# Moving four memory-token products within the written-out order of a transformer kernel

## The chip, the cores and the metric

The kernel runs on one core of one Trainium2 chip. The metric is the device time of one execution in microseconds (us). The core has five engines that each work through their own instruction stream in program order: PE (TensorE, matrix products), DVE (VectorE), ACT (ScalarE), POOL (GpSimd) and SP (SyncE, here the queue that issues the loads). They meet only at semaphores.

## What is computed

A first block takes x (256 tokens, 1024 features): root-mean-square norm, one wide input projection, and three branches from it: a latent attention (8 heads, ranks 384 and 256, rotary part of 32), a decaying attention ("fox", 8 heads of 64) and a state-space scan (16 heads of 64, after a short convolution). Gates, an output projection and a convolved feed-forward follow. A second block of two layers follows, whose memory attention uses keys and values of 256 memory tokens. These depend on the inputs alone. In the reference:

```python
def memory_kv(mem, mem_norm, w_mem_kv):
    b, m, _ = mem.shape
    k, v = jnp.split(rmsnorm(mem, mem_norm) @ w_mem_kv, 2, axis=-1)
    return (k.reshape(b, m, N_MEM_HEADS, HEAD_DIM), v.reshape(b, m, N_MEM_HEADS, HEAD_DIM))
```

and the latent attention's up-projection, with the norm and the rotation of each head:

```python
    q = (rms_norm(c_q, q_norm_g) @ w_uq).reshape(Bsz, S, MLA_HEADS, MLA_QK_DIM)
    kv = (rms_norm(c_kv, kv_norm_g) @ w_ukv).reshape(Bsz, S, MLA_HEADS, MLA_NOPE + MLA_V)
    q = rope_tail(rms_norm(q, q_gain), cos, sin)
    k = rope_tail(rms_norm(k, k_gain), cos, sin)
```

Only the time at which the four memory products (keys and values of two layers) are formed is touched.

## The kernel before

Everything is held feature-major, 128 partitions by chunks times 256 tokens. The function `order` writes out one list of steps, `STEPS`. Every engine's program is a walk through that same list (L1079 for PE, L1431 for ACT, L1858 for DVE, L717 for SP), so the list fixes each engine's own order, and semaphores fix the rest. A step ("g", stage, i) is a product group, which fills one of four PSUM banks. The others are: "sq" squares on ACT, "ns" and "nm" the norm's sums on PE, its `Ln` and `Exp` on ACT and its application on DVE, "rope" the rotation (one product on PE, three DVE operations), "trig" the sine table (18 short dependent DVE operations in `angles_` at L1531, then a `Sin` on ACT at L1436 and the reload of the function table), "A", "B", "C", "D" the phases of an attention head.

Each group's weights, mostly 1 MB, come through `ring`, four slots (`load`, L693). SP issues the load of number n in the order of the list, and only once slot n - 4 is free. Two kinds of groups exist. For the stages in `SPLIT` (the input projections "min", "fqk", "fv", "xbc", "z" and others) the weights are first split into a high and a low part, `w_hi` on ACT (L1154) and `w_lo` on DVE (L1497), two buffers of each, and the product is three matmuls for one (`three`, L769, matmuls at L779). The slot is free once `w_lo` is made. For the rest ("uq", "uk", "uv", "memkv") the matmuls read `ring` itself (L810, L819, L874), and the slot is free only once the group is done.

Where a split stands in the streams of ACT and DVE is decided by `split_before` (L414): at the group in which its buffer comes free, that is at the last use of the split two before it. If the slot four loads back belongs to a group that isn't split, it stands no earlier than two groups behind that one:

```python
        g = LAST[BY_SPLIT[n - 2]] if n >= 2 else -1
        before = BY_LOAD.get(LOAD[key] - RING)
        if before is not None and before not in SPLITS:
            g = max(g, min(LAST[before] + 2, GROUP_OF[key] - 1))
```

In a group's turn ACT and DVE make the splits first and then empty the bank. For "xbc" the splits come behind the linear part and the taps of the convolution (L1214, L1609).

Around the change the list is: norms of x and of the memory, "min" 0 and 1 and "min2" (latent inputs), memory product 0, "trig", memory products 1 to 3, squares of the query latent ("sq cq"), "fqk" 0, its norm ("nm cq"), and so on through "fqk" 3 and "fv" 1, then the up-projection: ten groups "uq" 0 to 3, "uk" 0 to 3, "uv" 0 and 1 (variable `up`), with the norm of group t - 1 and the rotation of group t - 2 behind group t. After it come the fox heads, each with one "xbc" or "z" group behind it. On PE, "nm cq" waits for the squares of ACT, which stand behind "trig" in ACT's stream. The memory groups' banks are emptied by ACT (L1193), those of "uq" and "uk" by DVE (L1576).

Of the kernel before, what the change touches and what calls it, by code (L numbers as in the profile page):

```python
# [243 lines left out]
def order():  # L244

    def norm(name):  # L250

        return [(k, name, i) for i in range(4) for k in ("sq", "ns")] + [("nm", name)]

    def late(name, groups):


        per = len(groups) // 4
        out = []
        for i in range(4):
            out += groups[per * i:per * i + per] + [("sq", name, i)]  # L260
            if i:
                out.insert(len(out) - 1 - (per > 1), ("ns", name, i - 1))
        return out

    def down(n):
        return [("g", f"down{n}", c) for c in range(KC)]

    st = norm("x1") + [("g", "fdt", 0)]
    st += [("g", "min", 0), ("ft",)] + norm("mem") + [("g", "min", 1), ("g", "min2", 0)]
    st += [("g", "memkv", 0), ("trig",)] + [("g", "memkv", n) for n in range(1, 4)]  # L270
    st += [("sq", "cq"), ("g", "fqk", 0), ("nm", "cq"), ("sq", "ckv"), ("g", "fqk", 1), ("nm", "ckv")]
    st += [("sq", "f0"), ("g", "fqk", 2), ("nm", "f0"), ("sq", "f1"), ("g", "fqk", 3), ("nm", "f1")]
    st += [("sq", "f2"), ("g", "fv", 0), ("nm", "f2"), ("sq", "f3"), ("g", "fv", 1), ("nm", "f3")]

    up = [("g", "uq", n) for n in range(4)] + [("g", "uk", n) for n in range(4)]
    up += [("g", "uv", 0), ("g", "uv", 1)]
    for t, g in enumerate(up):
        st += [g] + ([("sq", f"m{t}")] if t < 8 else []) + ([("nm", f"m{t - 1}")] if 1 <= t <= 8 else [])
        st += [("rope", t - 2)] if t >= 2 else []

    def ticks(heads, fill):

        n = len(heads)
        out = [("G", *heads[0])]
        for t in range(n + 2):
            out += [("A", *heads[t])] if t < n else []
            out += [("D", *heads[t - 2])] if t >= 2 else []
            out += [("C", *heads[t - 1])] if 1 <= t <= n else []
            out += [("B", *heads[t])] if t < n else []
            out += [("E", *heads[t - 1])] if 1 <= t <= n else []  # L290
            out += [("G", *heads[t + 1])] if t + 1 < n else []
            out += fill(t)
        return out

    first = [("g", "xbc", n) for n in range(6)] + [("g", "z", n) for n in range(2)]
    st += ticks([("fox", h) for h in range(FOX_H)], lambda t: first[t:t + 1])
    st += [("cb", 0), ("cb", 1)]

    fill = [("g", "z", 2), ("g", "z", 3)] + [(("g", "gate", 4 + n), ("g", "brf", n))[m] for n in range(4) for m in (0, 1)]
    st += ticks([("mla", h) for h in range(8)], lambda t: fill[t:t + 1] + ([("xt", t)] if t < 4 else []))  # L300
    rest = [(("g", "gate", n), ("g", "brm", n))[m] for n in range(4) for m in (0, 1)]
    rest += [("g", "gate", n) for n in range(8, 12)]

    def ssd_fill(t):

        out = rest[t:t + 1]
        for i in range(4):
            if t == max(4 * i + 5, len(rest) + i):
                out += [("sq", "ssm", i)] + ([("ns", "ssm", i)] if i < 3 else [])
        return out  # L310

    st += ticks([("ssd", h) for h in range(SSM_H)], ssd_fill)
    st += [("g", "brs", 0), ("ns", "ssm", 3), ("nm", "ssm")] + [("g", "brs", n) for n in range(1, 4)]
    st += late("ffn1", [("g", "out1", n) for n in range(4)]) + [("nm", "ffn1"), ("ffn", "1")]
    st += late("mixa", down("1"))

    st += [("g", "qma", 0), ("ns", "mixa", 3), ("nm", "mixa")] + [("g", "pool", n) for n in range(4)]
    wg = [("g", "wg", n) for n in range(4)]
    st += ticks([("mema", h) for h in range(4)], lambda t: wg[t:t + 1])
    st += late("ffna", [("g", "outa", n) for n in range(KC)]) + [("nm", "ffna"), ("ffn", "a")]  # L320
    st += late("mixb", down("a"))

    st += [("g", "kk", 0), ("ns", "mixb", 3), ("nm", "mixb"), ("g", "qq", 0), ("rt",), ("g", "kv", 0)]
    more = [("g", "kk", 1), ("g", "qq", 1), ("g", "kv", 1), ("g", "kk", 2), ("g", "qq", 2),
            ("g", "kv", 2), ("g", "qmb", 0)]
    heads = [("sb", h) for h in range(12)] + [("memb", h) for h in range(4)]
    st += ticks(heads, lambda t: more[t:t + 1])
    st += late("ffnb", [("g", "outb", n) for n in range(4)]) + [("nm", "ffnb"), ("ffn", "b")]
    st += late("last", down("b")) + [("ns", "last", 3), ("nm", "last")]
    return st  # L330


STEPS = order()


# [1638 lines left out]
```

## Time and profile before

| what | value |
|---|---|
| median of 3 runs | 1327.72 us (1326.32 to 1330.77) |
| span of the profiled execution | 1326.9 us, 21884 instructions |
| PE busy | 1243.7 us, 94% |
| DVE busy | 745.5 us, 56% |
| ACT busy | 602.3 us, 45% |
| mean granted PE clock | 0.970 of full |

The span runs from the first to the last instruction of one execution. Busy times of PE are modelled at their ends, so that the pitch (start to start) of its groups tells more than the length of one. The page's chain of work follows back from the last instruction to what released each step.

### The profile page before, as it was taken

The page shows a single profiled execution, that of the slowest core. Times are in us where ns is not written, and L with a number is a line of the kernel's source. Part 1 is how long each engine was busy: PE and PEld are TensorE (multiplying, and loading weights), DVE is VectorE, ACT ScalarE, POOL GpSimd, SP SyncE. Part 2 cuts the span into 40 slices and gives each one's busy share as a digit, 9 for nine tenths or more (in the row PEclk, how much of TensorE's full clock was granted, in tenths as well). Part 3 has the DMA queues.
Part 4 walks back from the last instruction along what each step waited for, and adds up shares of the span by engine and source line. Part 5 has one row for each costly group of instructions (what it writes and reads, how often), then busy time and mean ns, then how long its engine had stood idle before and what let it go on. Part 6 is the DMA issues. An engine that isn't in the chain of part 4 may idle for free.

```text
span 1326.9 us, 21884 instructions
## 1 busy us (share of the span) xinstructions
PE 1243.7 (94%) x8910; PEld 1138.8 (86%) x8910; DVE 745.5 (56%) x1167; ACT 602.3 (45%) x930; POOL 127.8 (10%) x118
## 2 busy tenths in 40 slices
PE   5899899889997999998998999999999989999996
PEld 4798378778896999888997799999999758999996
DVE  3424678543544768887547247775555333677643
ACT  4346355443333565554451254444566633544333
POOL 0000011000432015554000000000000000000000
PEclk8899899999998999999998999999999979999998
DMA  7152143213351444444551265544554104555451
GB/s 270 67 204 92 53 152 103 96 49 143 124 194 64 155 161 163 158 164 134 173 182 51 90 232 191 183 159 160 194 194 145 43 1 147 203 188 179 134 180 49
DMA packets 29789, 186.56 MB, mean 141 GB/s; under 512 B 3312, under 2 KB 3568, under 8 KB 13456
## 3 DMA queue, kind: packets, MB, share of 16 engines
q1 hardware_dynamic: 29712, 185.46, 40.0%
q8 instruction: 57, 0.93, 0.3%
q14 instruction: 20, 0.16, 0.0%
HBM read 184.40 MB, written 1.05 MB: 140 GB/s over the span
## 4 chain that ended last, share of the span: by engine, by line
PE 76%; DVE 9%; ACT 7%; issue 6%; DMA 1%; DVEq 0%; ACTq 0%; POOL 0%; POOLq 0%; SPq 0%
PE bank L779 54%; PE bank L810 6%; DVE acc L1832 3%; ACT w_hi L1154 3%; PE bank L909 3%; DVE w_lo L1497 3%; PE S L959 2%; PE O L1071 2%; PE T L1045 1%; PE bank L819 1%; PE O L1075 1%; ACT xh L1266 1%; PE S L1014 1%; PE S L1038 1%; PE S L986 1%
## 5 line engine op out<-in xcount | busy, mean ns | idle before, releaser
L1497 DVE TENSOR_TENSOR w_lo<-ring,w_hi 128x1024 fp32r<-128x1024 f32 (+4 forms) x338 | 369.1, 1133 | 281.3 <-ACT w_hi L1154 281.2
L779 PE MATMUL bank<-xh,w_hi 128*128 128x256 f32 (+2 forms) x1736 | 496.5, 286 | 16.1 <-DVE w_lo L1497 7.7
L779 PE MATMUL bank<-xl,w_hi 128*128 128x256 f32 (+2 forms) x1736 | 488.8, 282 | 0.0
L779 PE MATMUL bank<-xh,w_lo 128*128 128x256 f32 (+2 forms) x1736 | 488.6, 281 | 0.0
L1154 ACT ACTIVATE w_hi<-ring 128x1024 fp32r<-128x1024 f32 (+4 forms) x338 | 309.5, 964 | 348.3 <-PE bank L779 343.8
L779 PEld LDWEIGHTS bank<-xh,w_hi 128*128 128x128 f32 (+2 forms) x1736 | 325.9, 188 | 23.2 <-issue 14.7
L779 PEld LDWEIGHTS bank<-xl,w_hi 128*128 128x128 f32 (+2 forms) x1736 | 326.0, 188 | 0.9 <-issue 0.2
L779 PEld LDWEIGHTS bank<-xh,w_lo 128*128 128x128 f32 (+2 forms) x1736 | 325.8, 188 | 0.4
L779 PE MATMUL bank<-hid_hi,w_hi 128*128 128x256 f32 x528 | 150.8, 286 | 3.0 <-POOL hid_lo L1932 2.1
L779 PE MATMUL bank<-hid_lo,w_hi 128*128 128x256 f32 x528 | 149.0, 282 | 0.0
L779 PE MATMUL bank<-hid_hi,w_lo 128*128 128x256 f32 x528 | 148.9, 282 | 0.0
L779 PEld LDWEIGHTS bank<-hid_hi,w_hi 128*128 128x128 f32 x528 | 100.3, 190 | 3.7 <-POOL hid_lo L1932 2.3
L779 PEld LDWEIGHTS bank<-hid_lo,w_hi 128*128 128x128 f32 x528 | 100.3, 190 | 0.2
L779 PEld LDWEIGHTS bank<-hid_hi,w_lo 128*128 128x128 f32 x528 | 100.3, 190 | 0.0
L1822 DVE TENSOR_TENSOR acc<-bank,rstd 128x512 f32<-128x512 f32 x44 | 30.4, 691 | 48.4 <-PE bank L779 48.4
L959 PE MATMUL S<-sqr,cst 128*128 128x256 f32 x128 | 37.9, 434 | 16.5 <-ACT sqr L1285 16.5
L1266 ACT ACTIVATE xh<-x,cst,par 128x256 fp32r<-128x256 f32 x40 | 21.8, 592 | 64.3 <-DVE x L1652 35.1
L1832 DVE SCALAR_TENSOR_TENSOR acc<-pr,par,acc 128x255 f32<-128x255 f32 (+1 forms) x88 | 46.5, 568 | 3.0 <-DVE acc L1832 0.2
L959 PEld LDWEIGHTS S<-sqr,cst 128*128 128x128 f32 x128 | 26.7, 221 | 20.9 <-issue 9.7
L1415 ACT ACTIVATE sg<-acc,cst 128x256 f32<-128x256 f32 x22 | 11.2, 510 | 62.9 <-DVE acc L1832 62.9
L1932 POOL TENSOR_TENSOR hid_lo<-sg,hid_hi 128x256 f32 (+1 forms) x22 | 32.2, 1464 | 3.5 <-POOL hid_hi L1930 3.4
L1652 DVE TENSOR_TENSOR x<-x,bank 128x256 f32<-128x256 f32 x32 | 13.3, 416 | 31.9 <-PE bank L909 25.3
(262 smaller groups left out, 1570.1 us busy)
## 6 DMA issues: line engine op xcount, KB each, us to landing
ring<-w_up SPq DMA_DIRECT2D x22, 1024.0 KB, 4.8
ring<-w_upa SPq DMA_DIRECT2D x22, 1024.0 KB, 4.9
ring<-w_upb SPq DMA_DIRECT2D x22, 1024.0 KB, 4.9
ring<-w_gate SPq DMA_DIRECT2D x12, 1024.0 KB, 5.7
ring<-w_down SPq DMA_DIRECT2D x16, 704.0 KB, 4.2
ring<-w_downa SPq DMA_DIRECT2D x16, 704.0 KB, 4.1
ring<-w_downb SPq DMA_DIRECT2D x16, 704.0 KB, 4.1
ring<-w_xbc SPq DMA_DIRECT2D x6, 1024.0 KB, 4.9
```

What stands on the lines that cost most here:

```text
L779: last = mm(out, lhs, rhs, start=(k == 0 and (a, b) == (0, 0)), stop=(whole and k == ks[-1] and (a, b) == (1, 0)))
L810: last = mm(b[p0:p0 + width, m * S:m * S + S], W[0:kp, k * wide + c0:k * wide + c0 + width], src(k), start=(k == 0), stop=(k == kc - 1))
L909: last = mm(banks[g % RING][:, 0:S], W[0:p, k * P:(k + 1) * P], src, start=(k == 0), stop=(k == 9))
L959: last = mm(b[:, 0:S], C("ones"), sqr[:, ((i % 2) * 2 + c) * S:((i % 2) * 2 + c + 1) * S], start=(i == 0 and c == 0), stop=(i == 3 and c = ...
L1071: mm(o[:, 0:S], v[:, 0, :], p[:, 0:S], start=True, stop=False)
L1154: A(w_hi[:, q % 2, a:e], raw[:, a:e], ACT.Copy).then_inc(hi_ready, 1)
L1266: last = A(hi[:, c, :], src[:, c, :], ACT.Identity, bias=C("zero"), scale=Pm(gain, c))
L1497: last = V.tensor_tensor(w_lo[:, q % 2, a:e], raw[:, a:e], w_hi[:, q % 2, a:e], ALU.subtract)
L1652: V.tensor_tensor(x[:, i, :], x[:, i, :], b[:, 0:S], ALU.add).then_inc(free, 1)
L1822: V.tensor_tensor(y.rearrange("p (a t) -> p a t", a=2), bank[:, :].rearrange("p (a t) -> p a t", a=2), factor(S), ALU.mult).then_inc(free, 1)
L1832: ins = stt(part, y[:, m * S:(m + 1) * S - late], par[:, bass.ds(j * 8 + o, 1)], part, ALU.mult, ALU.add)
L1932: Q.tensor_tensor(lo, h, hi, ALU.subtract).then_inc(up_hid, 1)
```

## The change

The four memory groups leave their place between "min2" and "sq cq", and only "trig" stays there. They stand now in the up-projection, one behind the rotation step of every even t below 8, that is behind "uq" 0, "uq" 2, "uk" 0 and "uk" 2. Nothing is added or removed.

```diff
     st += [("g", "min", 0), ("ft",)] + norm("mem") + [("g", "min", 1), ("g", "min2", 0)]
-    st += [("g", "memkv", 0), ("trig",)] + [("g", "memkv", n) for n in range(1, 4)]
+    st += [("trig",)]
     st += [("sq", "cq"), ("g", "fqk", 0), ("nm", "cq"), ("sq", "ckv"), ("g", "fqk", 1), ("nm", "ckv")]
@@
     for t, g in enumerate(up):
         st += [g] + ([("sq", f"m{t}")] if t < 8 else []) + ([("nm", f"m{t - 1}")] if 1 <= t <= 8 else [])
         st += [("rope", t - 2)] if t >= 2 else []
+        st += [("g", "memkv", t // 2)] if t % 2 == 0 and t < 8 else []
```

Load numbers, ring slots, bank numbers and the places of the splits follow from the list by the same functions.

## Rows read from the trace of the kernel before

**Rows 1.** The page: its span, and its chain by engine.

```profile
span 1326.9 us, 21884 instructions
...
PE 76%; DVE 9%; ACT 7%; issue 6%; DMA 1%; DVEq 0%; ACTq 0%; POOL 0%; POOLq 0%; SPq 0%
```

**Rows 2.** Stretches of 10 us: busy time (instructions) by engine, PE clock, DMA share, GB/s.

```profile
140.00:150.00 10.00, 7.08 (x18) 2.57 (x18) 5.91 (x8) 3.68 (x6) 0.00 (x0) 0.73 0.22 91
...
260.00:270.00 10.00, 8.81 (x61) 8.43 (x62) 3.31 (x9) 3.62 (x10) 0.00 (x0) 0.83 0.32 105
```

**Rows 3.** Chain of work in order of time, 0 to 200 us: start, length, what.

```profile
57.61 6.91 PE bank L810 x32
...
85.23 5.63 PE bank L779 x48
90.86 1.29 PE S L760 x6
...
125.04 5.19 PE bank L810 x24
...
147.53 0.69 DVE mqk L1576
...
153.20 0.69 DVE mqk L1576
...
171.90 0.97 PE S L1092 x2
...
183.44 5.63 PE bank L779 x48
```

**Rows 4.** Timeline of the up-projection, PE: start, length, line, tiles.

```profile
135.43 2.83 PE L810 MATMUL bank<-xbc,ring 128*96 128x256 f32 x12
...
138.10 1.02 PE L974 MATMUL S<-sqr,cst 96*96 96x512 f32 x2
...
139.06 1.04 PE L1092 MATMUL S<-mqk,cst 32*32 32x512 f32 x2
...
140.03 1.94 PE L810 MATMUL bank<-xbc,ring 128*64 128x256 f32 x8
```

**Rows 5.** Timeline of DVE: first and last of 18 angle operations, one split.

```profile
50.72 0.42 DVE L1536 CAST acc<-sg 32x512 f32<-32x512 int32 x1
...
60.06 0.42 DVE L1554 TENSOR_SCALAR merged<-merged 32x512 f32<-32x512 f32 x1
...
98.98 2.36 DVE L1497 TENSOR_TENSOR w_lo<-ring,w_hi 128x1024 fp32r<-128x1024 f32 x2 [3.25 <-ACT w_hi L1154]
```

**Rows 6.** Timeline of ACT: the sine, squares of the query latent, one split.

```profile
65.17 1.28 ACT L1436 ACT_TABLE_LOAD   x1
66.46 1.14 ACT L1436 ACTIVATE merged<-merged,cst 32x1024 f32<-32x1024 f32 x1
67.62 1.28 ACT L1135 ACT_TABLE_LOAD   x1
...
85.77 0.93 ACT L1280 ACTIVATE sqr<-xbc,cst 128x768 f32<-128x768 f32 x1
...
97.88 2.01 ACT L1154 ACTIVATE w_hi<-ring 128x1024 fp32r<-128x1024 f32 x2 [1.34 <-PE bank L779]
```

**Rows 7.** Timeline of ACT behind the first state-space group.

```profile
183.77 1.28 ACT L1216 ACT_TABLE_LOAD   x1
```

**Rows 8.** Timeline of DVE behind the first state-space group: taps, then a split.

```profile
181.97 2.69 DVE L1604 SCALAR_TENSOR_TENSOR acc<-bank,halves,acc 128x255 f32<-128x255 f32 x6 [3.65 <-ACT acc L1211]
184.57 2.35 DVE L1497 TENSOR_TENSOR w_lo<-ring,w_hi 128x1024 fp32r<-128x1024 f32 x2
```

**Rows 9.** Timeline of PE: its restart after an idle stretch.

```profile
39.55 6.73 PE L959 MATMUL S<-sqr,cst 128*128 128x256 f32 x16 [5.13 <-ACT sqr L1285]
```

**Rows 10.** Stretches of 1 us, PE: length, busy (instructions), granted clock, DMA share, GB/s.

```profile
39.00:40.00 1.00, 0.45 (x1) 0.50 0.69 270
...
45.00:46.00 1.00, 1.00 (x6) 0.66 0.00 0
```

**Rows 11.** Loads issued from 78 to 86 us: count, KB each, median us to landing.

```profile
ring<-w_fqk SPq DMA_DIRECT2D x2, 1024.0 KB, 4.9
ring<-w_fv SPq DMA_DIRECT2D x1, 1024.0 KB, 7.0
```

## The prediction, as it was put on record before the kernel ran

> **What bounds the kernel now.** I read the page's chain first. PE holds 76% of a span of 1326.9 us, and DVE, ACT and issue share nearly all the rest [rows 1]. So a change pays where PE isn't the one that is waited for. The chain in order of time gives those places for the stretch that is edited. From 57.61 to 85.23 it is PE alone, back to back: the four memory products, 6.91 us each [rows 3]. Then "fqk" and "fv" follow without a wait (5.63 us a group, 1.29 for the sums of "nm cq"), until the up-projection starts at 125.04 [rows 3]. There the chain leaves PE. It goes round through DVE's emptying of a bank, ACT's square, `Ln` and `Exp`, DVE's scaling and its three rotation operations, and back to the next emptying: 147.53 to 153.20 is one turn, 5.67 us [rows 3]. The stretches agree: from 140 to 150 PE was busy for 7.08 of 10 us, at a granted clock of 0.73 [rows 2]. The last rotation is at 171.90, 0.97 long, so the up-projection lasts 172.87 - 125.04 = 47.8 us [rows 3]. This is the idle time of PE that the change fills. Four things have to be priced.
>
> **1. What leaves the front.** The memory products were on the chain for 85.23 - 57.61 = 27.6 us [rows 3]. Without them "fqk" 0 can start at 57.61. Its weights are there: the loads of "fqk" take the ring turns that the memory loads had, and these were issued long before. Its split now stands at "min" 1 (its slot and its buffer are free by then), so `w_lo` is made well before 57.61. Gain: -27.6.
>
> **2. What the memory products covered.** They stood beside "trig". Now "trig" has two splits ahead of it on DVE and only one group of PE beside it. DVE's stream is static: split of "fqk" 0 at "min" 1, split of "fqk" 1 at "min2", and then the angles. The second waits for the product of "min2", which still reads the buffer, so it begins at 57.61. A split takes 3.46 us from the start of `w_hi` to the end of `w_lo` (97.88 on ACT to 98.98 + 2.36 on DVE) [rows 5, 6], so the angles start at 61.07 instead of 50.72. They take 60.48 - 50.72 = 9.76 us [rows 5] and end at 70.83. ACT then has the sine, 1.14, the reload of its table, 1.28, and the squares of the query latent, 0.93 [rows 6]: 74.2. With a semaphore's 0.1 PE gets its sums "nm cq" at 74.3. It had finished "fqk" 0 at 57.61 + 5.63 = 63.24, and "nm cq" is next in its stream, ahead of "fqk" 1. **PE stands still for 11.1 us.** Queued behind ACT's wait for the angles are those squares, the split of "fqk" 2 and the emptying of "fqk" 0; none of them is later than PE once PE moves again. The first of the two table loads I count as hidden: at 183.77 ACT began such a load although the taps that its `Tanh` waits for ended only at 181.97 + 2.69 = 184.66 [rows 7, 8], so a load is made ahead of the wait. Were it behind the wait, 1.3 us more.
>
> The Trainium skill's page ScalarE: Activation LUTs ("What ACT_TABLE_LOAD costs") gives about 2.66 us for a switch, a drain included. The trace doesn't bear out the drain, for the sine follows its load by 0.01 us [rows 6]; by the page the sum would be 1.4 us more for the reload.
>
> Then the clock. After an idle time of 5.13 us PE restarted at 39.55, with a granted clock of 0.50 [rows 9, 10], that is 1.2 GHz, and had 2.4 GHz again in the course of the stretch 45 to 46 (0.66) [rows 10]. That is 6.2 us at half speed, 3.1 us lost. An idle time of 11.1 us is longer, so I take the same loss, with 0 and 3.4 as ends. Cost of part 2: +11.1 + 3.1 = +14.2.
>
> **3. The up-projection with the memory products in it.** First PE's work alone, by pitches at full clock. "uq" takes 138.10 - 135.43 = 2.67, a norm's sums 139.06 - 138.10 = 0.96, a rotation 140.03 - 139.06 = 0.97, "uk" about 1.90 [rows 4], "uv" the same. The sum is 4 x 2.67 + 6 x 1.90 + 8 x 0.96 + 8 x 0.97 + 4 x 6.91 = 65.2 us. This is above 47.8: PE becomes the bound, and the idle time takes up only 10.2 of the 27.6 us.
>
> Then what PE still waits for, from its start at 0, by the same durations. While "uq" goes, nothing: each memory product gives the DVE and ACT turn more than its 5.67 us. "uq" 3 ends at 27.4. It frees a ring slot, so memory load 3 is issued and right behind it that of "xbc" 0, at 27.75. Two loads that close landed after 4.9 and 7.0 us [rows 11], so "xbc" 0 is there at 34.8. Its split now stands in the turn of "uk" 0, ahead of the emptying of that bank (two groups behind memory product 1, whose slot it takes). ACT waits there for the load, and behind it on ACT are the squares of "uk" 0 and the norm before it, on DVE the emptying of "uk" 0. The split ends at 38.25. Emptying, square, `Ln`, `Exp` and scaling (0.7 each) end at 41.9 and the first rotation operation at 42.6. PE meanwhile has "uk" 0, sums, a rotation and memory product 2, until 40.05, and "uk" 1 until 41.95. So this wait of some 5 us is nearly all covered. Going on, PE waits 0.3 us for the sums behind "uk" 2 and 1.25 us for the rotation before memory product 3, as the turn of "uk" 1 has no product beside it; near the end 0.2 more. In all 1.9 us, and 67.1 us for the stretch: 67.1 - 47.8 = **+19.3**. Bounds: 65.2 with no wait (+17.4), and 2.6 us more where "xbc" 0 lands later (9.6 us, had two loads been ahead of it), +22. PE is then busy for 65.2 of 67.1 us, more than in either stretch of [rows 2] where the clock fell, so I keep its full clock.
>
> **4. The fox heads' start.** Before, the split of "xbc" 1 lay in the up-projection's turn. Now its load waits for the slot of the "uk"/"uv" weights, free at the end of "uv" 1, and `split_before` puts its split at "xbc" 0, behind the taps. There the trace has a split already (of "xbc" 2): taps at 181.97, `w_lo` from 184.57 to 186.92 [rows 8]. That place is taken by "xbc" 1's. PE was at "xbc" 1 at 183.44 [rows 3], so it now waits 186.9 - 183.4 = **+3.5 us**. The load, issued a little ahead of 172.9 in the old time, lands by about 179, before ACT wants it at 181.8. "xbc" 2's split follows, 2.35 later, and PE wants it only 9 us on. Ends: 0, if DVE's order left room (it doesn't), and +1.7 more if the idle time lets the clock fall for a while, as in the stretch 260 to 270, with PE busy for 8.81 us and a clock of 0.83 [rows 2] (1.7 of 10 us, twice, at half speed). From "xbc" 3 on, loads, splits and banks stand as before, so the rest only shifts.
>
> **Sum.** -27.6 + 14.2 + 19.3 + 3.5 = +9.4 us. On the profiled execution: 1326.9 + 9.4 = 1336.3. The median of the runs shown is 0.8 above that span, so the prediction is **1337.1 us**, 0.7% slower.
>
> **The rivals.**
> - *The clock costs nothing at the restart, or less.* Then +6.3 us, 1334.0. Against it: the restart at 39.55. Chance 0.12.
> - *The middle is worse.* ACT's wait for "xbc" 0 comes out through PE, because the loads share the DMA engines with memory load 3 (+2.6), the clock falls once there or at "xbc" 1 (+1.7), and the sine's table load is behind the wait (+1.3): +15.0, 1342.7. For it: three small bounds that all point one way. Chance 0.15.
> - *Faster: PE isn't held at "nm cq".* This is the one mechanism that changes the sign. The angles, sine, reload and squares take 9.76 + 1.14 + 1.28 + 0.93 + 0.1 = 13.2 us, and hide if they start by 63.2 - 13.2 = 50.0. With part 2 at nothing the sum is -27.6 + 19.3 + 3.5 = -4.8, 1322.9. It needs the angles to be ahead of both splits on DVE; in the list they are behind "min2". Chance 0.07.
> - *The change does what it says in full:* the up-projection stays at 47.8 us, with its idle time holding all products. Then -27.6 + 14.2 + 3.5 = -9.9, 1317.8. PE's own 65.2 us speak against it. Chance 0.02.
>
> The forecast has 0.62; 0.02 are left for what I don't see.
>
> **How the numbers follow.** The forecast's own bounds (clock 0 to 3.4, up-projection +17.4 to +22, fox start up to +5.2, table load 0 to 1.3) reach from about 1332 to 1343, and the first two rivals lie inside. The range is 1330 to 1343; outside it are the two faster cases and small tails. What a measurement of this kernel can tell from no change is about 0.3%, 4 us. Faster by more has the last rival and nearly all of the one before it: 0.07. Within 0.3%, that is up to 1331.7, needs most of the bounds at their low ends at once, or a part of the stall at "nm cq" gone: 0.10. Slower has 0.83.
>
> **What would show it.** In the profile of the changed kernel PE should stand idle for 11 us before the sums of "nm cq" (L760), near 63 to 74 us, released by ACT's squares; the angles on DVE should start near 61. The granted clock should be 0.50 for some 6 us after that. From the first "uq" to the first fox scores it should be near 67 us, with PE busy nearly throughout, ACT waiting for the load of "xbc" 0 by the split's line, and the memory products at 6.9 us each. At the second "xbc" group there should be an idle time of 3.5 us, released by `w_lo`. The prediction is wrong if the angles are ahead of the splits on DVE, if the up-projection is far from 67 us, or if a later stage changes its length by more than 1 us.

## The result and the profile after

| | kernel before | changed kernel |
|---|---|---|
| median of 6 runs each | 1328.99 us | 1339.74 us (1337.68 to 1346.26) |
| ratio | | 1.009, 95% interval 1.006 to 1.012 |
| span of the profiled execution | 1326.9 us | 1338.2 us |
| mean granted PE clock | 0.970 | 0.966 |

The change makes the kernel slower by 0.9%, 10.8 us by the medians. 1337.1 us was forecast, which is 9.4 us above the median of 1327.72 us that the kernel before had at that time; three more runs of it brought that median to 1328.99. The spans differ by 11.3 us. All line numbers of kernel.py behind the edit are one higher than before. The page has PE's share of the chain as it was [rows 1]:

```profile
span 1338.2 us, 21884 instructions
...
PE 76%; DVE 10%; ACT 7%; issue 5%; DMA 1%; DVEq 0%; ACTq 0%; POOL 0%; SPq 0%; POOLq 0%
```

The chain of work in order of time, 0 to 205 us (start, length, what), answers to [rows 3]:

```profile
44.69 11.35 PE bank L780 x96
56.12 1.07 ACT w_hi L1155
57.22 2.36 DVE w_lo L1498 x2
59.61 0.43 DVE acc L1537
...
68.95 0.43 DVE merged L1555
70.56 1.28 ACT L1136
71.86 0.94 ACT sqr L1281
72.84 2.93 PE S L761 x6
75.77 6.57 PE bank L780 x48
82.34 0.86 PE S L761 x4
...
109.41 12.09 PE bank L811 x56
...
175.99 0.42 PE S L999 x2
...
190.21 7.41 PE bank L780 x48
```

PE ends "min2" at 44.69 + 11.35 = 56.04. The chain then leaves PE: it goes through the split of "fqk" 1, the angles, the sine, the reload of the table and the squares, and comes back to PE only at 72.84. "fqk" 0 isn't on it at all. From there PE holds it up to the up-projection, which lasts from 109.41 to 175.99, 66.6 us against 47.8 before.

The timeline of PE has the two idle times and who ended them, in the brackets at the end of each line:

```profile
72.84 2.93 PE L761 MATMUL S<-sqr,cst 128*128 128x256 f32 x6 [11.18 <-ACT sqr L1281]
...
190.21 0.42 PE L780 MATMUL bank<-xh,w_hi 128*128 128x256 f32 x1 [3.63 <-DVE w_lo L1498]
```

The timeline of ACT has both waits that the prediction named, for the angles and for the load of "xbc" 0:

```profile
60.31 1.28 ACT L1437 ACT_TABLE_LOAD   x1
69.40 1.14 ACT L1437 ACTIVATE merged<-merged,cst 32x1024 f32<-32x1024 f32 x1 [7.81 <-DVE merged L1555]
...
143.79 2.01 ACT L1155 ACTIVATE w_hi<-ring 128x1024 fp32r<-128x1024 f32 x2 [4.45 <-DMA ring<-w_xbc]
```

Here the sine's table load, at 60.31, ends 7.8 us ahead of the sine itself: a load is made ahead of the wait, as [rows 7, 8] let expect. The stretches of 1 us of PE (length, busy, granted clock, DMA share, GB/s) answer to [rows 10]:

```profile
64.00:65.00 1.00, 0.00 (x0) 0.53 0.00 0
...
77.00:78.00 1.00, 1.00 (x8) 0.64 0.85 230
...
189.00:190.00 1.00, 0.00 (x0) 1.00 0.00 0
190.00:191.00 1.00, 0.79 (x4) 0.68 0.00 0
191.00:192.00 1.00, 1.00 (x7) 0.50 0.77 205
...
193.00:194.00 1.00, 1.00 (x7) 0.61 1.01 393
```

The clock went to 1.2 GHz (0.50) some 2.4 us into the long idle time, which began at 61.7, and was back at 2.4 GHz only behind 77. Behind the short idle time it fell too, in the stretch from 190 to 191 in which PE restarted, and was back behind 193.

### The profile page after: what moved, and what is told of

The parts are those of the page before. It is cut to its first block, busy times and chain, and to the rows that moved or that the text cites. A ratio compares the mean times of both kernels' runs of the same rounds, so it can differ in the third digit from the quotient of the medians.

```text
span 1338.2 us, 21884 instructions
## 1 busy us (share of the span) xinstructions
PE 1244.0 (93%) x8910; PEld 1142.4 (85%) x8910; DVE 745.5 (56%) x1167; ACT 602.9 (45%) x930; POOL 128.9 (10%) x118
## 4 chain that ended last, share of the span: by engine, by line
PE 76%; DVE 10%; ACT 7%; issue 5%; DMA 1%; DVEq 0%; ACTq 0%; POOL 0%; SPq 0%; POOLq 0%
PE bank L780 54%; PE bank L811 6%; DVE acc L1833 3%; DVE w_lo L1498 3%; ACT w_hi L1155 3%; PE bank L910 3%; PE S L960 2%; PE O L1072 2%; PE bank L820 1%; PE T L1046 1%; PE O L1076 1%; PE S L1015 1%; ACT xh L1267 1%; PE S L1039 1%; PE S L975 1%
## 5 line engine op out<-in xcount | busy, mean ns | idle before, releaser
L1416 ACT ACTIVATE sg<-acc,cst 128x256 f32<-128x256 f32 x22 | 11.2, 511 | 62.7 <-DVE acc L1833 62.7
```

## The experiments

Each time is a median, each ratio is to the kernel before, run on the same chip, and the brackets behind a ratio are its 95% interval. The diffs show edits against the changed kernel (for e5 and e7: against e1); "..." marks what is left out.

**e1_trig_early** moves the sine step ahead of "min" 1 and with it the application of the memory's norm behind "min" 1. It leaves the memory products where the change put them.

```diff
-    st += [("g", "min", 0), ("ft",)] + norm("mem") + [("g", "min", 1), ("g", "min2", 0)]
-    st += [("trig",)]
+    st += [("g", "min", 0), ("ft",)] + norm("mem")[:-1] + [("trig",), ("g", "min", 1)]
+    st += [("nm", "mem"), ("g", "min2", 0)]
```

> The changed kernel, but the sine table's step is put between the memory norm's last sums and min 1, and the memory norm's application behind min 1, so that on DVE the 18 angle operations stand ahead of both splits and in a stretch in which DVE has nothing to do (about 40 to 47 us). My theory (PE stands still for 11.2 us at the sums of nm cq because ACT's squares wait behind the sine and the sine behind the angles, and then loses 2.6 us of clock): both go, and the time falls by about 13.8 us against the changed kernel, to 0.998 of the kernel before. Rival (the 11 us are owed to the weights of fqk, which the memory products gave time to be split): the wait stays and is released by w_lo, time within 3 us of the changed kernel, 1.008.

Measured: 1322.79 us, ratio 0.9959 (0.9931 to 0.9986). DVE's timeline has the first angle operation at 40.13, and the chain (start, length, what) runs through the place of the idle time on PE:

```profile
46.47 16.96 PE bank L780 x144
63.43 1.29 PE S L761 x6
64.73 5.70 PE bank L780 x48
...
97.61 12.09 PE bank L811 x56
...
178.38 7.49 PE bank L780 x48
```

"min" 1, "min2" and "fqk" 0 are 144 matmuls without a gap, the sums of "nm cq" follow at once, at full clock (1.29 us against 2.93). From the restart at 46.47 to the start of the sums are 16.96 us, against 72.84 - 44.69 = 28.15 in the changed kernel: the 11.2 us are gone. The rival falls. With the sine's cost removed the change gains. By the ratios this kernel is 1.3% (17 us) below the changed one where 13.8 us had been expected; the two intervals cover the difference.

**e6_one_product_left** is the same cause in another dose.

```diff
-    st += [("trig",)]
+    st += [("g", "memkv", 0), ("trig",)]
...
-        st += [("g", "memkv", t // 2)] if t % 2 == 0 and t < 8 else []
+        st += [("g", "memkv", t // 2)] if t in (2, 4, 6) else []
```

> The changed kernel with one memory product left in its old place ahead of the sine step, the other three behind uq 2, uk 0 and uk 2. My theory: that product gives PE 6.9 us of work while the angles run, so the idle time at the sums of nm cq shrinks from 11.15 to about 4.2 us, us for us, and the clock loss of 2.6 us behind it mostly goes; the up-projection gets 6.9 us shorter, less about 0.5 for the turn of uq 0; the idle time at xbc 1 stays at 3.65 us. That is -6.9 (idle) -2.6 (clock) and +0.5: 8 to 9 us below the changed kernel, 1.002 to 1.003 of the kernel before. Rival (the idle time has a fixed cause): it stays near 11 us.

Measured: 1328.83 us, ratio 1.0033 (1.001 to 1.0056). The timeline of PE:

```profile
74.13 2.93 PE L761 MATMUL S<-sqr,cst 128*128 128x256 f32 x6 [4.28 <-ACT sqr L1281]
```

6.91 us of work put back took 11.18 - 4.28 = 6.90 us from the idle time. The clock part of the expectation was wrong: the sums still took 2.93 us, so an idle time of 4.28 us cost as much clock as one of 11.18. This is the plainest test of what the products covered, since one product moved back is its whole edit. The up-projection took 59.7 us (60.2 expected).

**e4_block_before_up** keeps the front and undoes the interleaving.

```diff
+    st += [("g", "memkv", n) for n in range(4)]
     up = [("g", "uq", n) for n in range(4)] + [("g", "uk", n) for n in range(4)]
...
-        st += [("g", "memkv", t // 2)] if t % 2 == 0 and t < 8 else []
```

> The changed kernel without the interleaving: all four memory products in one block directly ahead of the first uq group. The front is as in the changed kernel, the up-projection as in the kernel before, and the slot order of xbc as before. My theory: only the front's 13.8 us are left as a cost, about 1.010 to 1.011 of the kernel before, with an up-projection of 47.8 us and no idle time at xbc 1; so the interleaving by itself gains 27.6 - 18.75 = 8.85 us and gives 5.4 back at xbc 1, and this kernel is about 2.5 to 3 us slower than the changed one. Rival (interleaving gains nothing, because a turn with a product in it makes ACT and DVE late): this kernel is as fast as the changed one or faster.

Measured: 1342.27 us, ratio 1.010 (1.0063 to 1.0138). Its chain:

```profile
111.03 6.91 PE bank L811 x32
...
138.68 4.75 DMA ring<-w_xbc
...
189.43 0.42 PE S L999 x2
...
200.02 5.70 PE bank L780 x48
```

Block and up-projection last from 111.03 to 189.43, 78.4 us, against 66.6 interleaved. So the interleaving takes 11.8 us off, more than the 8.85 expected, since the block has a cost that I had overlooked: "xbc" 0 now follows memory product 3 in its slot, and ACT waits for that load in the turn of "uq" 1 with nothing beside it. As expected, the second "xbc" group starts 200.02 - 189.43 = 10.6 us behind the first fox scores and not 14.2. The times don't settle which of the two kernels is slower: they weren't run beside each other, and the intervals of their ratios (1.0063 to 1.0138, 1.006 to 1.012) overlap. The traced execution of e4 even ended at 1334.1 us, 4.1 us ahead of that of the changed kernel, though it was some 8 us behind when it ended "xbc" 1 (200.02 + 5.70 against 190.21 + 7.41). Its granted clock was higher later on, 0.93 against 0.76 between 1050 and 1100 us. So the 11.8 us are shown for that stretch, by one trace of each, and not in the time of the whole kernel.

**e2_products_earlier** asks what the idle time at "xbc" 1 comes from. Memory products 2 and 3 stand behind "uq" 3 and "uk" 2.

```diff
-        st += [("g", "memkv", t // 2)] if t % 2 == 0 and t < 8 else []
+        st += [("g", "memkv", (0, 2, 3, 6).index(t))] if t in (0, 2, 3, 6) else []
```

> The changed kernel, but memory products 2 and 3 behind uq 3 and uk 2 (steps t = 0, 2, 3, 6 instead of 0, 2, 4, 6). The uk/uv weights then load one turn later, and the slot that xbc 1 needs is that of memory product 2, free early: its split moves back into the up-projection. My theory (the 3.65 us of idle time at the second xbc group, and 1.8 us of low clock behind it, come from that slot): they go, -5.4 us, and the up-projection gets some 2.6 us longer, as its turns with uk 0 and uk 1 have no product beside them and one more split: -2.8 us in all against the changed kernel. Rival (the wait at xbc 1 is DVE's load in the fox heads, wherever the slot comes from): no change there, +2.6 us.

Measured: 1343.06 us, ratio 1.0108 (1.0067 to 1.0148), a miss. Its chain, then the timeline of PE in its up-projection, then that of DVE in the fox heads:

```profile
163.97 9.55 PE bank L820 x32
...
194.62 5.71 PE bank L780 x48
204.18 2.28 DVE w_lo L1498 x2
206.59 7.39 PE bank L780 x48
```

```profile
159.84 1.07 PE L975 MATMUL S<-sqr,cst 96*96 96x512 f32 x2 [2.52 <-ACT lnv L1307]
```

```profile
204.09 4.63 DVE L1498 TENSOR_TENSOR w_lo<-ring,w_hi 128x1024 fp32r<-128x1024 f32 x4
```

The idle time at "xbc" 1 is gone (194.62), but one of the same kind stands at "xbc" 2, which is the one that now follows the uk/uv weights in their slot. The rule of `split_before` puts that split two groups behind "uv" 1, together with that of "xbc" 3 (four halves in one row). And the up-projection took 72.4 us, 5.8 more than in the changed kernel, where 2.6 had been expected: two turns without a product, those of "uk" 0 and "uk" 1, let PE idle, the clock fell, and memory product 3 took 9.55 us, not 7.1. The rival, which had seen no change at "xbc" 1, falls all the same.

**e3_both** has the edits of e1 and e2.

> Both edits: the sine table's step early, and the memory products at t = 0, 2, 3, 6. If both theories hold and the two add, -16.6 us against the changed kernel: 0.996 to 0.997 of the kernel before. If only the first holds, 0.999 to 1.000; if neither, 1.010.

Measured: 1329.51 us, ratio 1.0008 (0.9983 to 1.0032). This is near what had been expected if only the first theory holds (0.999 to 1.000). It is 13.5 us below e2, where the sine's part was put at 13.8. In the trace the sums of "nm cq" have no idle time, as in e1, and the up-projection takes 72.3 us, as in e2 (72.4). So the two parts don't disturb each other; against e1 the time is 6.7 us higher by the medians.

**e5_tail** frees the uk/uv slot early in another way, on top of e1.

```diff
-    up += [("g", "uv", 0), ("g", "uv", 1)]
+    between = {0: ("g", "memkv", 0), 2: ("g", "memkv", 1), 5: ("g", "uv", 0), 6: ("g", "uv", 1)}
...
-        st += [g] + ([("sq", f"m{t}")] if t < 8 else []) + ([("nm", f"m{t - 1}")] if 1 <= t <= 8 else [])
+        st += [g, ("sq", f"m{t}")] + ([("nm", f"m{t - 1}")] if t else [])
...
-        st += [("g", "memkv", t // 2)] if t % 2 == 0 and t < 8 else []
+        st += [between[t]] if t in between else []
+    st += [("g", "memkv", 2), ("nm", "m7"), ("rope", 6), ("g", "memkv", 3), ("rope", 7)]
```

> e1_trig_early with the up-projection laid out anew: memory products 0 and 1 behind uq 0 and uq 2, the two value groups uv behind uk 1 and uk 2 (they have no norm of their own and so fill turns), memory products 2 and 3 behind uk 3 with the last norm and the last two rotations between and behind them. The slot of the uk/uv weights is then free two groups before xbc 0, and the split of xbc 1 moves to memory product 3. My theory (the idle time at the fox heads' start follows the slot of xbc 1 and split_before's two groups): no idle time at xbc 1 or xbc 2, which saves 3.65 us and 1.8 us of low clock; the up-projection gets 2 to 4 us longer, since the uk turns have less beside them. 1 to 3.5 us below e1_trig_early, 0.993 to 0.995 of the kernel before. Rival (any split more in the up-projection costs as much there): 0.996 to 0.998.

Measured: 1325.2 us, ratio 1.0006 (0.9987 to 1.0026). Timeline of PE, then the chain:

```profile
135.64 1.99 PE L976 MATMUL S<-sqr,cst 96*96 96x512 f32 x2 [5.46 <-ACT lnv L1308]
```

```profile
123.01 6.97 DMA ring<-w_xbc
...
173.44 5.69 PE bank L781 x48
181.77 5.63 PE bank L781 x48
190.99 5.70 PE bank L781 x48
```

No idle time at "xbc" 1 or 2 (pitches 8.3 and 9.2 us, as before). But the up-projection took 75.6 us, 9.0 more than the 66.6 of e1, where 2 to 4 had been expected, and so the time is a miss (0.993 to 0.995 expected). What had covered ACT's wait for the load of "xbc" 0 was memory product 2 behind "uk" 0. Without it the load stands on the chain and the wait comes out on PE, 5.46 us, with a low clock behind it. This supports, from the other side, the cover in part 3 of the prediction; e5 moves other groups too, so it isn't a test of that product alone.

**e7_split_free_first** leaves the order of e1 and changes only where the split of "xbc" 1 stands: in the turn of "xbc" 0, ahead of the emptying of the bank and not behind the taps. `splits` takes the list of splits as `keys` for it; DVE's stream has the same edit as ACT's. In the turns of the other "xbc" groups the rule moves nothing.

```diff
+def split_xbc(g, free):
+    return [key for key in SPLIT_AT.get(g, []) if (LAST[BY_SPLIT[SPLITS[key] - 2]] < g) == free]
...
-                if stage != "xbc":
-                    splits(GROUP[stage, i])
+                splits(GROUP[stage, i], keys=split_xbc(GROUP[stage, i], True) if stage == "xbc" else None)
...
-                        splits(GROUP[stage, i])
+                        splits(GROUP[stage, i], keys=split_xbc(GROUP[stage, i], False))
```

> e1_trig_early with one edit more: in the turn of an xbc group, a split whose buffer is free already (that of xbc 1, in the turn of xbc 0) stands ahead of the emptying of the bank, and only the others stay behind the taps. My theory (PE's 3.65 us of idle time at xbc 1 come from the place of its split behind taps that it doesn't depend on, and the low clock behind it from that idle time): w_lo of xbc 1 is ready by the end of the product of xbc 0, the idle time falls to 0 to 0.5 us, the up-projection stays at 66.6 us, and 4 to 5.4 us go against e1_trig_early: about 0.992 of the kernel before. Rival (the load of xbc 1, which waits for the slot of the uk/uv weights, lands too late): the idle time stays above 2 us, released by the DMA through w_hi.

Measured: 1319.61 us, ratio 0.9934 (0.9909 to 0.996). The timeline of DVE and the chain:

```profile
170.02 2.36 DVE L1502 TENSOR_TENSOR w_lo<-ring,w_hi 128x1024 fp32r<-128x1024 f32 x2 [0.20 <-ACT w_hi L1160]
173.26 2.69 DVE L1609 SCALAR_TENSOR_TENSOR acc<-bank,halves,acc 128x255 f32<-128x255 f32 x6 [0.88 <-ACT acc L1216]
```

```profile
166.46 5.63 PE bank L785 x48
174.73 5.70 PE bank L785 x48
184.01 5.70 PE bank L785 x48
```

The split is made while PE is still in "xbc" 0, and "xbc" 1 starts at 174.73, 8.3 us behind the start of "xbc" 0, at full clock. The load wasn't late: ACT had begun `w_hi` by 168.94. This version is faster than both kernels, by 0.7% against the kernel before.

**e1_again** ran on the same chip as e7.

> e1_trig_early once more on the chip of e7_split_free_first, so that the two can be compared at the same state. 0.996 of the kernel before, as it was. Idle time at xbc 1 3.65 us.

Measured: 1326.09 us, ratio 0.9971 (0.9947 to 0.9994). So e7's edit is worth some 5 to 6.5 us by the times (the ratios and the medians), 5.4 by the traces (idle time 3.6, product 7.45 against 5.70 us). The intervals of the two ratios overlap.

**before_again and after_again** give a second trace of each kernel.

> The kernel before once more, for a second trace. The trace of the changed kernel has 2.8 us more than the kernel before between 262 and 285 us, at identical work, where its granted clock is low for some 7 us more. If that belongs to the change, this trace shows the same clock there as the first (low for 3 us between 250 and 300). If it is chance, the low stretches differ from the first trace's, and the span with them.

> The changed kernel once more, for a second trace. Everything up to the second xbc group should repeat within 1 us (idle time of 11.15 us, up-projection of 66.6 us, idle time of 3.65 us). If the 2.8 us behind it are chance, the clock between 258 and 308 us is low for another length than the 10 us of the first trace.

Measured spans: 1321.3 and 1333.5 us, one execution each, against 1326.9 and 1338.2 in the first traces: both are some 5 us shorter at the same instructions. The difference of the two kernels is 12.2 us here and was 11.3. In after_again the up-projection, from 111.04 on, and the start of "xbc" 1, at 191.89 with 7.46 us, repeat the first trace. The start of "min" 1 doesn't: it was 1.6 us earlier in the changed kernel (44.69 against 46.28) and is 1.5 us later here (46.03 against 44.48). The stretch from 250 to 300 us (length, busy, clock, DMA share, GB/s), in before_again, after_again, e1_trig_early and e1_again, one fence each:

```profile
250.00:300.00 50.00, 43.47 (x298) 0.95 0.15 54
```

```profile
250.00:300.00 50.00, 41.05 (x273) 0.90 0.15 53
```

```profile
250.00:300.00 50.00, 43.46 (x303) 0.97 0.19 70
```

```profile
250.00:300.00 50.00, 43.46 (x279) 0.90 0.16 55
```

The two traces of the changed kernel agree (0.90 both), so they alone would have spoken for a cost of the change. The two traces of e1 don't: one kernel has 0.97 and 0.90 there. In all twelve traces of this case 0.90 stands in four: both of the changed kernel, e1_again and e6. The other eight have 0.93 to 0.97, among them the first of e1 and that of e7, which have the memory products in the same places. So the change doesn't fix the value, but it may well make the lower one more frequent; the runs leave this open.

What makes the second traces shorter lies mostly further on. The stretch from 1050 to 1100 us, in before, before_again, after and after_again:

```profile
1050.00:1100.00 50.00, 41.30 (x153) 0.80 0.00 0
```

```profile
1050.00:1100.00 50.00, 41.61 (x170) 0.86 0.06 21
```

```profile
1050.00:1100.00 50.00, 43.52 (x185) 0.76 0.00 1
```

```profile
1050.00:1100.00 50.00, 40.30 (x207) 0.93 0.02 7
```

The kernel before has 0.80 and 0.86 there, the changed one 0.76 and 0.93, each at nearly the same place in its work. So a few us of difference between two spans can come from there.

## Why the prediction was right

Point by point, changed kernel against kernel before, in us of the first profiled executions:

| step of the prediction | forecast | measured |
|---|---|---|
| 1. products out of the front | -27.6 | -27.6; "min2" also ended 1.6 earlier (56.04 against 57.61) |
| 2. PE idle at the sums of "nm cq" | +11.1 | +11.2 |
| 2. low clock behind it | +3.1 | +2.6 (72.84 to 82.34 is 9.5; 1.29 + 5.63 before [rows 3]) |
| 3. up-projection | +19.3 | +18.8 (66.6 against 47.8) |
| 4. PE idle at "xbc" 1 | +3.5 | +3.6 |
| 4. low clock behind it | 0, bound 1.7 | +1.8 (7.41 against 5.63) |
| the rest | 0 | +2.5 (remainder to 11.3); it arises between 250 and 300 us, with the low clock there |

**The mechanism of each term held.** The angles started at 59.61, 1.5 us ahead of the 61.07 forecast, because "min2" ended 1.6 earlier. The first table load was hidden. The reload took 1.28 us, and the squares began 0.02 us behind its end (70.56 and 71.86), so no drain is seen here either. ACT waited for the load of "xbc" 0, and product 2 covered it; e5 shows what it costs uncovered. The two bounds of step 3 (+17.4 and +22) hold the measured +18.8, near the lower: 66.6 us are 1.4 above PE's own 65.2, and not 1.9. The one wait of PE in the stretch is 1.2 us, for the rotation ahead of memory product 3, where the prediction had put 1.25; its two smaller waits, 0.3 and 0.2, didn't come.

**What was mis-sized is the clock.** I took full clock behind the idle time at "xbc" 1 and put the loss into a bound; it came in the changed kernel, in its second trace, and in both of e1. e6 adds that 4.28 us of idle time cost the full 2.6 too. With the measured 1.8 as the likeliest value the forecast would have been 1338.9, nearer to the 1339.74 measured; another 1.3 us is the median of the kernel before, which was 1327.72 with three runs and 1328.99 with six. The 1.6 us at the front come from ahead of the change: the restart of PE that [rows 9] show at 39.55 came at 38.45, and its sums took 6.24 us, not 6.73. They are chance, for the second pair of traces has the sign the other way (1.5 us later).

**One of its own signs of being wrong came true.** The prediction called itself wrong if a later stage changed its length by more than 1 us. In the first pair of traces the part behind "xbc" 1 is 2.8 us longer (1140.6 against 1137.8). In the second pair it is as long as before (1134.2 against 1134.0), though the clock between 250 and 300 us was the lower one again, because other stretches came out the other way. The work there is unchanged, so the sum didn't miss a step of the order; but that the total of 11.3 us came so near to the forecast of 9.4 rests in part on terms of the clock, between 1 and 3 us each, that partly cancel. The sign and the large terms (-27.6, +11.2, +18.8, +3.6) don't rest on them: they are the same in both pairs.

**The rivals.** The first (no clock loss at the restart) fell by the 0.50 in the stretches and the 2.93 us of the sums. The second, a worse middle, got one of its three bounds (the clock at "xbc" 1) and not the others. The third, faster, needed the angles ahead of both splits by 50.0: e1 builds just that order (angles from 40.13) and is faster, as its condition said, by a ratio of 0.9959 where -4.8 us, 0.9964, had been worked out. The fourth, the products all hidden, fell by PE's own work.

## What to carry to other kernels

Before work is moved out of a stretch, ask what it covered there: here 27.6 us of products hid a serial chain of 13 us on two other engines, and what the move of independent work into idle time elsewhere gained (27.6 - 18.8 = 8.8 us) was lost to it. In a list that orders all engines at once, what stands ahead in each engine's stream matters more than the place in the list; moving the chain to where its engines were idle, and a split ahead of work that it doesn't depend on, turned 1.009 into 0.993. Idle time of an engine can be filled only down to its own sum of work, so add that up first.

## What the runs showed of the hardware beyond that

- The loss behind an idle time of PE isn't in proportion to it: 11.18 us and 4.28 us were followed by the same 2.93 us for the six matmuls of the sums (1.29 at 2.4 GHz), and 3.63 us by 1.8 us of loss in the next group.
- Runs of one kernel differ by more than this change, and the granted clock goes with it: 28 runs of the kernel before on one chip went from 1320.96 to 1336.06 us, and these two had a mean granted clock of 0.976 and 0.963.
- The load of "xbc" 0, 1 MB and issued right behind another of 1 MB, landed 6.9 us after its issue in the changed kernel (136.87 to 143.76) and 7.0 in e5, as [rows 11] had it (7.0). In e4, where no load was issued right ahead of it, the chain has 4.75 us.
